# Gated delta core of a six-sublayer float32 block: the triangular inverse on compact 32x32 blocks instead of 64x64 ones

## The reference

```python
def _gated_delta_chunked(q, k, v, g, beta):
    ...
    decay = jnp.exp(jnp.where(causal, gc[..., :, None] - gc[..., None, :], -jnp.inf))
    kb = k * beta[..., None]
    lower = jnp.where(strict, jnp.einsum('nhcid,nhcjd->nhcij', kb, k) * decay, 0.0)
    rhs = jnp.concatenate([v * beta[..., None], kb * jnp.exp(gc)[..., None]], axis=-1)
    uw = lax.linalg.triangular_solve(lower, rhs, left_side=True, lower=True, unit_diagonal=True)
    u, w = uw[..., :dv], uw[..., dv:]
    ...
    def step(state, inp):
        u_c, w_c, qk_c, qg_c, kd_c, a_c = inp
        v_new = u_c - jnp.einsum('nhik,nhkv->nhiv', w_c, state)
        o = jnp.einsum('nhik,nhkv->nhiv', qg_c, state) + jnp.einsum('nhij,nhjv->nhiv', qk_c, v_new)
        state = state * a_c[..., None, None] + jnp.einsum('nhjk,nhjv->nhkv', kd_c, v_new)
        return state, o
```

## Time and profile before

| what | value |
|---|---|
| median of 3 runs | 3029.96 us (3028.45 to 3035.49) |
| the profiled execution's own time | 3024.55 us |
| its span, first to last instruction | 3022.7 us |
| PE busy | 2898.4 us |
| POOL, DVE, ACT busy | 1551.7, 1268.9, 1132.0 us |
| delta core, first `turned_blocks` to the end of the last unit | 653.3 to about 930 us |

### The profile page before, as it was taken

How to read it: one execution, slowest core, us unless ns; L and a number is a source line. 1 busy time by engine, 2 the same in 40 slices (tenths; PEclk the granted TensorE clock), 3 DMA queues, 4 the chain that set the end, 5 groups by cost and what they waited for, 6 DMA issues and landing times.

```text
span 3022.7 us, 52535 instructions
## 1 busy us (share of the span) xinstructions
PE 2898.4 (96%) x21626; PEld 2524.4 (84%) x21626; DVE 1268.9 (42%) x2575; ACT 1132.0 (37%) x1725; POOL 1551.7 (51%) x1243
## 2 busy tenths in 40 slices
PE   6999999999999999999999998899999999999998
PEld 4788778878887778887788876799988899888998
DVE  3221246765654421233212356523446552456552
ACT  2212223334333312213222145433455664465663
POOL 2344443422123344444354444688856788556786
PEclk8999999999999999999999999999999999999999
DMA  7433342210003223343242440254543445343453
GB/s 280 168 106 137 109 193 96 86 57 2 3 3 154 106 100 136 121 189 128 99 145 103 169 156 29 97 177 169 186 165 114 153 170 191 128 166 112 157 173 128
DMA packets 58914, 389.94 MB, mean 129 GB/s; under 512 B 6480, under 2 KB 7760, under 8 KB 21360
## 3 DMA queue, kind: packets, MB, share of 16 engines
q1 hardware_dynamic: 48896, 317.87, 29.7%
q10 hardware_dynamic: 9648, 68.32, 5.9%
q0 software_dynamic: 192, 1.25, 0.1%
HBM read 386.36 MB, written 1.05 MB: 128 GB/s over the span
## 4 chain that ended last, share of the span: by engine, by line
PE 69%; POOL 16%; issue 8%; DVE 4%; ACT 2%; DMA 1%; POOLq 0%; ACTq 0%; DVEq 0%
PE bank L685 18%; PE bank L687 18%; PE bank L686 18%; POOL ring_lo L2837 16%; PE bank L719 2%; PE bank L1349 1%; PE bank L1036 1%; PE bank L1071 1%; PE bank L1083 1%; DVE core L2742 1%; PE bank L1044 0%; DVE core L2686 0%; POOL core L2910 0%; PE bank L1369 0%; PE bank L1047 0%
## 5 line engine op out<-in xcount | busy, mean ns | idle before, releaser
L2837 POOL TENSOR_TENSOR ring_lo<-ring,w_hi 128x512 fp32r<-128x512 f32 (+1 forms) x832 | 1060.4, 1307 | 1032.7 <-ACT w_hi L1511 1032.6
L687 PE MATMUL bank<-h_hi,ring_lo 128*128 128x256 f32 (+1 forms) x3256 | 1074.8, 330 | 0.0
L685 PE MATMUL bank<-h_hi,w_hi 128*128 128x512 f32 (+1 forms) x2384 | 837.9, 351 | 30.2 <-POOL ring_lo L2837 21.4
L686 PE MATMUL bank<-h_lo,w_hi 128*128 128x512 f32 (+1 forms) x2448 | 844.5, 345 | 0.0
L687 PEld LDWEIGHTS bank<-h_hi,ring_lo 128*128 128x128 f32 x3256 | 622.5, 191 | 57.2
L1511 ACT ACTIVATE w_hi<-ring 128x2048 fp32r<-128x2048 f32 (+2 forms) x226 | 395.1, 1749 | 471.4 <-PE bank L687 382.1
L685 PEld LDWEIGHTS bank<-h_hi,w_hi 128*128 128x128 f32 x2384 | 453.9, 190 | 107.3 <-issue 24.8
L686 PEld LDWEIGHTS bank<-h_lo,w_hi 128*128 128x128 f32 x2448 | 466.8, 191 | 52.9
L687 PE MATMUL bank<-hid_r,ring_lo 128*128 128x256 f32 (+1 forms) x1088 | 363.9, 334 | 0.0
L2227 DVE SCALAR_TENSOR_TENSOR core<-core,bank 128x512 f32<-128x512 f32 (+1 forms) x88 | 54.7, 622 | 633.9 <-ACT core L1610 633.9
L685 PE MATMUL bank<-hid_r,w_hi 128*128 128x512 f32 (+1 forms) x808 | 285.6, 353 | 2.3 <-POOL ring_lo L2837 2.3
(11 more groups left out here) (437 smaller groups left out, 4240.9 us busy)
## 6 DMA issues: line engine op xcount, KB each, us to landing
ring<-w SPq DMA_DIRECT2D x88, 1024.0 KB, 4.8
ring<-up SPq DMA_DIRECT2D x48, 1024.0 KB, 4.8
ring<-w SPq DMA_DIRECT2D x64, 704.0 KB, 4.1
zbuf<-ada_later ACTq DMA_DIRECT2D x33, 1024.0 KB, 6.9
ring<-down SPq DMA_DIRECT2D x32, 768.0 KB, 4.3
core<-ada_later ACTq DMA_DIRECT2D x16, 1024.0 KB, 6.7
ring<-dn_in SPq DMA_DIRECT2D x16, 1024.0 KB, 4.8
ring<-mla_in SPq DMA_DIRECT2D x16, 1024.0 KB, 4.8
```

The source lines that it names most:

```text
L685: pe.matmul(out, a[0], b[0], start=start, stop=False)
L686: pe.matmul(out, a[0], b[1], start=False, stop=False)
L687: return pe.matmul(out, a[1], b[0], start=False, stop=stop)
L2837: ins = pool.tensor_tensor(like(ring_lo[:, r, a:b], part), like(ring[:, r, a:b], part), part.bitcast(F32), ALU.subtract)
```

## The change

The blocks are kept at 32x32 (`BK`), four in the four groups of 32 partitions (`BLOCKS`), so `X` and `XT` have 128 columns each instead of 256, and masks and identities are 32 wide. All steps up to the join of 16 to 32 (level 2) run on the four diagonal pieces 32*32 of the array: twice as many matmuls, each with a quarter of the area and half the moving columns. Level 3 is gone. In its place stands a join of 32 to 64 that looks like the last one: `pair_rows`, a negated copy on DVE (`pair_take`), `pair_update` in two parts, and two steps on DVE that put the results into 64-wide homes (`pair_seeing` into `XS`, `pair_seen` into `XTF`). ACT fills the rest of `XS` and `XTF` in a new step, `spread`: six copies of 32 partitions for each direction, ahead of `join_take`; the old `inverse` (two copies of 64 partitions each) is gone. `join_rows` and `join` stay at 64x64 and read `XS` and `XTF`; both wait for two semaphores. `near_blocks` takes four instructions of 32 partitions for a direction instead of two of 64. `lower` of direction 1 moves behind the pair join. The table of constants is 352 columns narrower.

```diff
-CONSTS = [("eps", 1), ("sel", 8), ("ident", 128), ("ones", 128), ("identc", 64), ("level", 2 * LEVELS * 64), ("incl", 2 * 128)]
+CONSTS = [("eps", 1), ("sel", 8), ("ident", 128), ("ones", 128), ("identc", BK), ("level", 2 * (LEVELS - 1) * BK), ("incl", 2 * 128)]
...
-            q["X"], q["XT"] = (xx[:, 256 * n:256 * n + 256].rearrange("p (h t) -> p h t", h=QUAD) for n in range(2))
-            q["XX8"] = xx.rearrange("p (g t) -> p g t", t=64)
+            q["X"], q["XT"] = (xx[:, 128 * n:128 * n + 128].rearrange("p (h t) -> p h t", h=QUAD) for n in range(2))
+            q["XX2"] = xx[:, 0:256]
+            q["XS"] = xx[:, 256:512].rearrange("p (h t) -> p h t", h=QUAD)
...
+        BLOCKS = [slice(BK * b, BK * b + BK) for b in range(4)]
+        NEAR_SEEN = [(BLOCKS[0], BLOCKS[2]), (BLOCKS[1], BLOCKS[3])]
+        NEAR_SEEING = NEAR_SEEN[::-1]
+        IN_SEEN = [list(zip(BLOCKS[0:2], BLOCKS[0:2])), list(zip(BLOCKS[2:4], BLOCKS[0:2]))]
...
                     for hd in range(QUAD):
-                        for r in HALVES if n < LEVELS - 1 else (SEEN[s],):
-                            pe.matmul(small4(s, C1, 0)[r, hd, :], q["XT"][r, hd, :], q["YL"][r, hd, :], start=True, stop=True)
+                        for r in BLOCKS:
+                            pe.matmul(small2(s, C1, 0)[r, hd, :], q["XT"][r, hd, :], q["YL"][r, hd, :], start=True, stop=True)
...
+                def pair_rows(U, s):
+                    q = quad[s]
+                    pe.wait_ge(dn["xu"][s], 5 * U + 3)
+                    for hd in range(QUAD):
+                        for seen, seeing in zip(NEAR_SEEN[s], NEAR_SEEING[s]):
+                            mm = pe.matmul(small2(s, C0)[seeing, hd, :], q[f"LT{U % 2}"][seen, hd, seeing], q["X"][seen, hd, :],
+                                           start=True, stop=True)
+                    mm.then_inc(dn["y"][s], 1)
+
+                def pair_update(U, s):
+                    q = quad[s]
+                    pe.wait_ge(dn["ym"][s], 5 * U + 5)
+                    seeing = NEAR_SEEING[s][s]
+                    for hd in range(QUAD):
+                        mm = pe.matmul(small2(s, C1, 0)[seeing, hd, :], q["XT"][seeing, hd, :], q["YL"][seeing, hd, :], start=True, stop=True)
+                    mm.then_inc(dn["z"][s], 1)
+                    for hd in range(QUAD):
+                        for seen, seeing in zip(NEAR_SEEN[s], NEAR_SEEING[s]):
+                            mm = pe.matmul(small2(s, C1, 1)[seen, hd, :], q["YL"][seeing, hd, :], q["XT"][seeing, hd, :],
+                                           start=True, stop=True)
                     mm.then_inc(dn["z"][s], 1)
...
                 def join_rows(U, s):
                     q = quad[s]
-                    pe.wait_ge(dn["xu"][s], 4 * U + 4)
+                    pe.wait_ge(dn["xu"][s], 5 * U + 4)
+                    pe.wait_ge(dn["inv"][s], 7 * U + 3)
...
-                    for n in range(1, LEVELS):
+                    for n in range(1, LEVELS - 1):
...
-                    for s in range(2):
-                        join_rows(U, s)
+                    for part in (pair_rows, pair_update, join_rows):
+                        for s in range(2):
+                            part(U, s)
...
+                def spread(U, s):
+                    q = quad[s]
+                    act.wait_ge(dn["xu"][s], 5 * U + 3)
+                    for r, t in IN_SEEN[s]:
+                        ins = act.activation(q["XS"][r, :, t], q["X"][r, :, :], ACT.Copy)
+                    ins.then_inc(dn["inv"][s], 1)
+                    for r in BLOCKS:
+                        ins = act.activation(q["XTF"][r, :, r], q["XT"][r, :, :], ACT.Copy)
+                    ins.then_inc(dn["inv"][s], 1)
...
-                    for part in (join_take, inverse, inverse_join, values_out):
+                    for part in (spread, join_take, inverse_join, values_out):
...
+                def pair_take(U, s):
+                    dve.wait_ge(dn["y"][s], 7 * U + 5)
+                    dve.tensor_scalar(quad[s]["YL"], small2(s, C0), -1.0, None, ALU.mult).then_inc(dn["ym"][s], 1)
...
-                    for n in range(1, LEVELS):
+                    for n in range(1, LEVELS - 1):
...
-                        elif n > 1 and more:
-                            lower(U + 1, n - 2)
+                        elif n == 2 and more:
+                            lower(U + 1, 0)
...
+                    for part in (pair_take, pair_seeing, pair_seen):
+                        for s in range(2):
+                            part(U, s)
                     if more:
+                        lower(U + 1, 1)
```

More of the change, by code:

```diff
@@ L212, in constants @@
         c[:, COFF["incl"] + 128 * s:COFF["incl"] + 128 * (s + 1)] = a <= b
-        for n in range(LEVELS):
+        for n in range(LEVELS - 1):
             m = DIAG << n >> 1
-            at = COFF["level"] + (s * LEVELS + n) * 64
+            at = COFF["level"] + (s * (LEVELS - 1) + n) * BK
             full = -1.0 * ((a // (2 * m) == b // (2 * m)) & ((b // m) % 2 == 0) & ((a // m) % 2 == 1))
@@ L218, in constants @@
                 full = -1.0 * ((a // DIAG == b // DIAG) & (a > b))
-            for r in range(2):
-                c[64 * r:64 * r + 64, at:at + 64] = full[64 * r:64 * r + 64, 64 * r:64 * r + 64]
-    c[:, COFF["identc"]:COFF["identc"] + 64] = np.tile(np.eye(64, dtype=np.float32), (2, 1))
+            for r in range(4):
+                c[BK * r:BK * r + BK, at:at + BK] = full[BK * r:BK * r + BK, BK * r:BK * r + BK]
+    c[:, COFF["identc"]:COFF["identc"] + BK] = np.tile(np.eye(BK, dtype=np.float32), (4, 1))
     return c
@@ L283, in level @@
         def level(s, n):
-            o = COFF["level"] + (s * LEVELS + n) * 64
-            return con[:, o:o + 64]
-        identc = con[:, COFF["identc"]:COFF["identc"] + 64]
+            o = COFF["level"] + (s * (LEVELS - 1) + n) * BK
+            return con[:, o:o + BK]
+        identc = con[:, COFF["identc"]:COFF["identc"] + BK]
         ident = con[:, COFF["ident"]:COFF["ident"] + 128]
@@ L412, in small4, with small2 @@
             return dwide[s][n][:, 256 * part:256 * part + 256].rearrange("p (h t) -> p h t", h=QUAD)
+        def small2(s, n, part=0):
+            return dwide[s][n][:, 128 * part:128 * part + 128].rearrange("p (h t) -> p h t", h=QUAD)
         def chunk_of(U, s):
@@ L985, in turned_blocks @@
                     if U >= 1:
-                        pe.wait_ge(dn["inv"][s], 5 * U)
+                        pe.wait_ge(dn["inv"][s], 7 * U)
                     for hd in range(QUAD):
-                        for r in HALVES:
-                            mm = pe.matmul(small4(s, C0)[r, hd, :], q[f"LT{U % 2}"][r, hd, r], identc[r, :], start=True, stop=True)
+                        for r in BLOCKS:
+                            mm = pe.matmul(small2(s, C0)[r, hd, :], q[f"LT{U % 2}"][r, hd, r], identc[r, :], start=True, stop=True)
                     mm.then_inc(dn["y"][s], 1)
@@ L1018, in diagonals @@
                     q = quad[s]
-                    pe.wait_ge(dn["xu"][s], 4 * U + 1)
+                    pe.wait_ge(dn["xu"][s], 5 * U + 1)
                     for hd in range(QUAD):
-                        for r in HALVES:
-                            pe.matmul(small4(s, C1, 0)[r, hd, :], q["XT"][r, hd, :], q["X"][r, hd, :], start=True, stop=True)
+                        for r in BLOCKS:
+                            pe.matmul(small2(s, C1, 0)[r, hd, :], q["XT"][r, hd, :], q["X"][r, hd, :], start=True, stop=True)
                     for hd in range(QUAD):
-                        for r in HALVES:
-                            mm = pe.matmul(small4(s, C1, 1)[r, hd, :], q["X"][r, hd, :], q["XT"][r, hd, :], start=True, stop=True)
+                        for r in BLOCKS:
+                            mm = pe.matmul(small2(s, C1, 1)[r, hd, :], q["X"][r, hd, :], q["XT"][r, hd, :], start=True, stop=True)
                     mm.then_inc(dn["z"][s], 1)
@@ L1030, in seen_rows @@
                     if n == 1:
-                        pe.wait_ge(dn["inv"][s], 5 * U + 2)
+                        pe.wait_ge(dn["inv"][s], 7 * U + 2)
                     else:
-                        pe.wait_ge(dn["xu"][s], 4 * U + n)
+                        pe.wait_ge(dn["xu"][s], 5 * U + n)
                     for hd in range(QUAD):
-                        for r in HALVES:
-                            mm = pe.matmul(small4(s, C0)[r, hd, :], q[f"LT{U % 2}"][r, hd, r], q["X"][r, hd, :], start=True, stop=True)
+                        for r in BLOCKS:
+                            mm = pe.matmul(small2(s, C0)[r, hd, :], q[f"LT{U % 2}"][r, hd, r], q["X"][r, hd, :], start=True, stop=True)
                     mm.then_inc(dn["y"][s], 1)
@@ L2018, in join_take @@
                     act.activation(quad[s]["YJ"][SEEING[s], :, :], small4(s, C0)[SEEING[s], :, :], ACT.Copy, scale=-1.0).then_inc(dn["inv"][s], 1)
-                def inverse(U, s):
-                    q = quad[s]
```

(8 more changed lines are left out.)

74 lines of the change are left out of this document (45 added, 29 removed).

## The result

The changed kernel takes 3085.06 us (median of 4 runs, 3082.83 to 3087.19) against 3029.87 before in the same session: ratio 1.0181, interval [1.0168, 1.0193]. It is 55 us slower where 45 us less were forecast. The profiled execution has a span of 3083.0 us and a clock of 0.957 (before 0.982).

A forecast was written before the change was run, and what follows sets the result against it. PE's stream of passes, alternating with PE-DVE chains, was taken as the bound. Eight units gave -54 us, the clock took back 9, net 45: 2980 against 3024.55, or 2985 from the median 3029.96; range 2965 to 3020.

The forecast's parts named there:

- the price of a pass: PE's small matmuls: 0.059 us per pass on a 64*64 piece, 0.030 on a 32*32 piece, four pieces side by side.
- Rival 2: Slower: the array starts no more than one pass in 0.029 us; 3112 us, chance 0.11.
- rival 1: Piece's price stays 0.059 us: 3011 us; half-way cases, large clock loss or late instructions 3002 to 3024; chance 0.18.
- a price by columns: PE's passes: 128 columns take 0.118 us, twice 64's 0.059, so price follows columns and 32 take 0.030.
- Start to the first `seen_rows`, odd: Odd unit's opening groups, turned_blocks, squares, fourths and diagonals, get shorter: -2.7 of 10.99 us.
- Level 1, odd: Odd unit's level 1, now bound by the chain of PE and DVE: 2.1 against 3.15 us, -1.0.
- Level 2, odd: Odd unit's level 2, with key_key (1.98 us) staying in it: 4.1 against 5.47 us, -1.4.
- From there to `new_values`, odd: Odd unit from level 3 to new_values, with key_query inside and PE the bound: 6.3 against 8.09 us, -1.8.
- `new_values` to the next unit: nothing: Unit's end: no gain; 6 to 10 us of 128x128 work hides lower of direction 1 and near_blocks.
- The other prices: DVE and ACT steps: 128 columns from PSUM 0.29 us on DVE, 0.27 on ACT; a spread copy 0.30.
- The clock: Core: 27 more microseconds at the low level, added to 27 before, cost 9 us, between 0 and 27.
- a level less at the end: Unit's end: a whole level of 3.4 us turns into a shorter one; even units -2.0 us to new_values.

The follow-up runs named there:

- e1: Separate kernel of matmul stretches only, without the computation or waits inside; 128 passes on four 32*32 pieces came every 3.46 us, about half the distances 3.73.
- e11: Kernel before, 64x64 layout, each small matmul up to level 3's updates split into two of 32 columns, doubling passes; 3175.66 us, ratio 1.0493, no stalls.
- e8: Changed kernel with ACT's order altered in odd units: spread and join_take ahead of the next unit's keep_keys; 3069.27 us, ratio 1.0142.
- e2: Changed kernel with its matmuls on 32*32 pieces cut to bfloat16, one pass each instead of two; 2998.5 us, ratio 0.9895.
- e7: Kernel before, 64x64 layout, with the inverse's small matmuls cut to bfloat16, one pass each; control of e2; 2994.42 us, ratio 0.9885.
- e5: Kernel before with ACT's order altered in even units: each direction's inverse, then its join_take, no compact blocks; 3021.20 us, ratio 0.9976.
- e9: e2's kernel (compact blocks, bfloat16 small matmuls) with e8's order on ACT in odd units; 2985.02 us, ratio 0.9859.
- e12: e7's kernel (64x64 layout, bfloat16 small matmuls) with e5's order on ACT in even units; 2993.83 us, ratio 0.9886.
- e4: Kernel before with only level 3 replaced by the pair join of 32 to 64, and lower of direction 1 behind it; 3033.94 us, ratio 1.0016.
- e10: e2's kernel plus two unread bfloat16 filler matmuls with each small group from level 1 to the join; 3026.62 us, ratio 0.9993.
- e3: Changed kernel plus two unread bfloat16 filler matmuls behind each wait from level 1 on; 3114.63 us, ratio 1.0283.

## Why the prediction was wrong

The main step that failed is **the price of a pass**. I bounded it by 0.059 us for a piece that doesn't get cheaper and by "0.029 us for each pass of the whole array", and took 0.030 for a piece, that is 0.0075 for the array. As the price of a burst it was right (32 passes in 0.45 us). As a rate it was not: e1 shows 128 passes in 3.46 to 3.73 us for every kind of short pass that was tried on four pieces. Rival 2 had this number; I put it at 0.11 because "0.029 is two pieces and not a limit of its own". Both are true: two 64*64 pieces take 0.0293 (e11, e1), and the supply, a different limit, lies only 3 to 8% below, at 0.027 to 0.028 on average. So in a long dense stretch of small matmuls there were under 10% to be had, not a half, and the change doubled the passes. Late instructions were named in rival 1, but priced as a loss of part of the gain, without counting: 1040 passes a unit at 0.027 are 28 us, and the forecast had units of 22 to 31.

Rival 2 said +82 and 55 came, since the supply is not a limit from pass to pass: it works ahead while PE waits or does 128x128 passes of 0.118 us, and then over a hundred passes can go at the speed of a burst. So the loss is that of the dense stretches: 53 us marked issue. The argument for a price by columns was wrong as well: in the rows that gave my price, the size of the piece and the number of moving columns changed together, and e11 halves the columns for nothing. The 0.45 us for pieces with both halved came out right by that luck.

**The sum, by its terms**, forecast and measured in the units shown. Start to the first `seen_rows`, odd: 8.3, measured 14.2 (780.51 to 794.69), 4.3 of it stalls. Level 1, odd: 2.1, measured 2.8 with its groups at the low clock. Level 2, odd: 4.1, measured 8.0: `key_key` at 3.78, a stall of 1.10. From there to `new_values`, odd: 6.3, measured 14.4: 4.7 of waits for `spread`, `key_query` at 3.78. These four are 20.8 us of forecast and 39.4 measured. The even unit 2, from 740.02 to `new_values` at 771.34, took 31.3 us where 20.7 were forecast, with four stalls of 0.9 to 1.8 us in its stream, its level 1, its level 2 and its pair join. The line "`new_values` to the next unit: nothing" looked for what hides `lower` of direction 1 and found PE's work; it did not follow who waits for `lower`, on ACT. That is the missed wait, 13.3 us of rows and 16 us by e8. (A slip that changes nothing: the terms of the even unit add up to -6.6 and not -6.7.)

**The other prices** held. Groups of the changed kernel (count, busy us, mean ns, idle before), to be read beside the earlier trace rows:

```profile
L2785 DVE TENSOR_TENSOR core<-bank,core 128x256 f32<-128x256 f32 x32 | 13.5, 423 | 30.6 <-PE bank L1057 30.2
...
L2769 DVE TENSOR_TENSOR core<-bank,con 128x128 f32<-128x128 f32 x48 | 13.2, 288 | 35.0 <-PE bank L1046 34.4
...
L2055 ACT ACTIVATE core<-core 32x128 f32<-32x128 f32 x32 | 9.8, 305 | 45.8 <-DVE core L2785 45.5
```

`masked` 288 ns (forecast 0.29), `update` 423 (0.42), a copy of `spread` 305 (0.30). DVE and ACT idle more than before: they were not the limit.

**The clock**: forecast 54 us at the low level and a cost of 9; measured 167 us of the core. Much of that lies in waits and stalls, where the clock costs nothing. It can be counted in the 128x128 groups (655 to 990 us):

```profile
L969 PE MATMUL bank<-big 128*128 128x128 f32 x64 | 13.5, 395 | 0.5 <-ACT core L2032 0.5
...
L953 PE MATMUL bank<-big 128*128 128x128 f32 x51 | 11.8, 422 | 0.0
```

At 2.05 us for 16 passes the first would be 8.2 and the second 6.5, 10.6 us less; the other groups on the whole array, by line against the trace of before, add some 7, of which `head_sums` (L963) is 3.8, 11.7 against 7.9. So about 18 us. The small groups at the low level come on top where PE is the bound (32 passes in 0.65 instead of 0.45 us) and were not priced. The mechanism was right, its size not. Stalls are not needed for it: in e2, with 7 us of stalls left, 118 of 238 us are at the low level, and in e7, with 64x64 blocks and no stall, 99 of 234, against 24 in the kernel before. What the low level would cost without stalls was not measured.

**The account** of the 52 us in the core: about 53 of stalls, 13 of waits for `spread` and 18 of clock are 84, so the smaller steps still gave some 32, by difference only. The pairs of runs point the same way: with the order mended compact blocks are 39 us slower in float32 than the kernel before (e8) and 48 slower than e5, which has its own order mended; with half of the passes they are 9 us faster (e9 against e12).

The forecast's second source, a level less at the end, is worth nothing by itself (e4, 5 us slower), and the place where ACT's `inverse` leaves the end of the chain, which I had priced within the change, is worth 8 us without it (e5).

## What to carry to other kernels

Before making TensorE's pieces smaller, count instructions: where a stretch of passes already starts one each 0.03 us, smaller pieces couldn't go faster for long here, and four pieces of 32 that needed twice the passes lost. Then follow each instruction that a change pushes back on one engine through the others' queues: who waits for it, and what stands behind the waiting one. And when a change moves an order together with a layout, price the order alone first; here it was the only part that paid.

## What the runs showed of the hardware

- PE gets about 256 instructions (128 passes with their weight loads, about one packet of 16.4 KB) in 3.45 to 3.73 us in the stalled stretches of e1, with 32 or 4 columns, in float32 or bfloat16; in the changed kernel it is 3.45 to 4.02 us, with 3.45 seen at a granted clock of 1.00 and of 0.50. Two of the stretches of e1 ran for 183 and 143 passes before the first stall, two others for 15. A packet itself took 0.9 to 1.4 us; why the next burst comes so late was not tried.
- In bursts four 32*32 pieces run side by side: 32 float32 passes in 0.45 us, and at the low clock level 128 bfloat16 passes in 1.22 us, where one piece takes 3.57.
- The price of a float32 pass in a 64*64 piece is 0.059 us with 64 columns and with 32; on four 32*32 pieces at the low clock 128 passes take 1.93 us with 32 columns and 1.88 with 4.
- Fillers of some 0.1 us behind each wait did not keep the clock up: 117 us of the core at the low level with them and 118 without (e10, e2), 134 and 167 in the changed kernel (e3).
